# Which buffer slots the first expert weights take at the start of the mixture-of-experts stage

## The reference

```python
def first_block(...):
    ...
        mix = jnp.concatenate([o_gla, o_moba, o_mem], axis=-1)
        x = x + jnp.einsum('bse,ed->bsd', mix, w_out[l])
        x = x + hierarchical_moe(rmsnorm(x, ffn_norm_g[l]), w_router_group[l], b_router_group[l],
                                 w_router_expert[l], b_router_expert[l], w_gate[l], w_up[l], w_down[l])

    def expert_block(args):
        toks, e = args
        xb = x_pad[toks]
        hid = jax.nn.silu(xb @ w_gate[e]) * (xb @ w_up[e])
        return hid @ w_down[e]
```

## Time and profile before

| | us |
|---|---|
| median of 3 runs | 1449.39 |
| lowest and highest | 1448.79, 1451.52 |
| the profiled execution, its own time | 1451.52 |
| the profiled execution, its span | 1449.8 |
| PE busy | 1186.8 (82%) |
| DVE busy | 616.1 (42%) |
| ACT busy | 475.5 (33%) |
| mean granted TensorE clock | 0.883 |

### The profile page before, as it was taken

How to read it: one execution, slowest core, us unless ns; L and a number is a source line. 1 busy time by engine, 2 the same in 40 slices (tenths; PEclk the granted TensorE clock), 3 DMA queues, 4 the chain that set the end, 5 groups by cost and what they waited for, 6 DMA issues and landing times.

```text
span 1449.8 us, 19467 instructions
## 1 busy us (share of the span) xinstructions
PE 1186.8 (82%) x7703; PEld 875.1 (60%) x7703; DVE 616.1 (42%) x1240; ACT 475.5 (33%) x767; POOL 7.6 (1%) x54
## 2 busy tenths in 40 slices
PE   5888878667565674666887789999999888999998
PEld 5665575233232341324664438899898745999986
DVE  4564742101000010002853676655445656665543
ACT  5552611000000000002622345544433456454541
POOL 1000000000000000000000000000000000000000
PEclk9997888888897897886997678999999988999999
DMA  8543668999999999999455432965454571756520
GB/s 298 182 168 104 245 232 335 430 429 429 429 430 429 429 431 428 431 420 341 146 177 188 158 117 97 287 198 175 175 199 179 207 272 45 233 178 201 201 90 30
DMA packets 121777, 368.68 MB, mean 254 GB/s; under 512 B 9890, under 2 KB 56141, under 8 KB 110926
## 3 DMA queue, kind: packets, MB, share of 16 engines
q1 hardware_dynamic: 120604, 367.26, 66.1%
q10 hardware_dynamic: 1074, 0.08, 0.1%
HBM read 366.28 MB, written 1.05 MB: 253 GB/s over the span
## 4 chain that ended last, share of the span: by engine, by line
PE 59%; DMA 20%; DVE 12%; ACT 4%; issue 3%; SPq 1%; DVEq 0%; ACTq 0%
PE ps L1832 57%; DMA more<-in_w_up_dram 8%; DMA more<-in_w_gate_dram 6%; DMA more<-in_w_down_dram 6%; DVE st L32 2%; DVE ring_r L32 2%; PE ps L1836 2%; DVE R_c L32 2%; SPq L669 1%; DVE X_c L32 1%; DVE R_a L32 1%; DVE X_a L32 1%; ACT X_c L32 1%; DVE sc L32 1%; ACT R_a L32 1%
## 5 line engine op out<-in xcount | busy, mean ns | idle before, releaser
L1832 PE MATMUL ps<-ring,xg 128*32 128x512 f32 x640 | 141.1, 741 | 125.4 <-DMA more<-in_w_gate_dram 78.3
L1832 PE MATMUL ps<-hT_r,ring_r 128*128 128x256 f32 x864 | 243.5, 282 | 0.0
L1832 PEld LDWEIGHTS ps<-ring,xg 128*32 128x32 f32 x640 | 37.3, 133 | 222.2 <-issue 222.2
L1832 PEld LDWEIGHTS ps<-hT_r,ring_r 128*128 128x128 f32 x864 | 165.8, 192 | 0.0
L32 DVE TENSOR_TENSOR ring_r<-ring,W_c_r 128x1024 fp32r<-128x1024 f32 x94 | 115.2, 1226 | 96.3 <-ACT W_c_r L32 92.4
L1832 PE MATMUL ps<-R_c_r,W_c_r 128*128 128x256 f32 x608 | 152.7, 283 | 0.0
L32 DVE TENSOR_TENSOR ring_r<-ring,X_c_r 128x1024 fp32r<-128x1024 f32 x88 | 107.8, 1225 | 95.2 <-ACT X_c_r L32 92.3
L1832 PE MATMUL ps<-R_c_r,X_c_r 128*128 128x256 f32 x576 | 147.7, 284 | 0.0
L1832 PE MATMUL ps<-more,xg 128*32 128x512 f32 x384 | 135.6, 727 | 0.0
L32 ACT ACTIVATE W_c_r<-ring 128x1024 fp32r<-128x1024 f32 x94 | 99.7, 1060 | 87.3 <-PE ps L1832 82.9
L32 ACT ACTIVATE X_c_r<-ring 128x1024 fp32r<-128x1024 f32 x88 | 93.3, 1061 | 89.5 <-PE ps L1832 84.3
(11 more groups left out here) (280 smaller groups left out, 1899.8 us busy)
## 6 DMA issues: line engine op xcount, KB each, us to landing
ring<-in_ada_w_dram SPq DMA_DIRECT2D x24, 2048.0 KB, 8.1
ring<-in_w_gate_dram SPq DMA_DIRECT2D x20, 2048.0 KB, 16.2
ring<-in_w_up_dram SPq DMA_DIRECT2D x20, 2048.0 KB, 18.5
ring<-in_w_down_dram SPq DMA_DIRECT2D x20, 2048.0 KB, 17.6
more<-in_w_gate_dram SPq DMA_DIRECT2D x12, 2048.0 KB, 26.4
more<-in_w_up_dram SPq DMA_DIRECT2D x12, 2048.0 KB, 27.5
more<-in_w_down_dram SPq DMA_DIRECT2D x12, 2048.0 KB, 26.3
ring<-in_ffn_gate_dram SPq DMA_DIRECT2D x22, 1024.0 KB, 5.9
```

The costliest lines, as they stand in the source:

```text
L1832: return pe.matmul(out, lhsT, rhs, start=start, stop=stop, skip_group_check=True)
```

## The change

The list that hands out slots is no longer written out at load 12 but derived from the rotation as it stands there. At that point `order` is [2, 3, 4, 0, 1]. The list before was [2, 0, 1, 5, 3, 4, 6, 7]; the new expression gives [4, 0, 1, 5, 2, 3, 6, 7].

```diff
@@ -380,7 +380,7 @@
         last_in = {}
         for k in range(nload):
             if k == m0:
-                order = [2, 0, 1, NR, 3, 4] + list(range(NR + 1, NR + MR))
+                order = order[2:] + [NR] + order[:2] + list(range(NR + 1, NR + MR))
             if k == m1_ + 1:
                 order = [z for z in order if z < NR]
             z = order.pop(0)
```

## The result

The changed kernel takes 1463.09 us (median of 4 runs, 1461.24 to 1464.96), the kernel before 1449.87 us beside it. The ratio is 1.0094, with a 95% interval of 1.0073 to 1.0115: it is slower by 13.6 us, between 10.6 and 16.7; the two medians are 13.2 us apart. The forecast was 1461.8 us in a range of 1459.0 to 1466.5. Of all 31 executions of the changed kernel 30 lie between 1461.24 and 1470.54 us with a median of 1462.6, and one, in a slow state with a mean granted clock of 0.70, took 1596.32 us and is left out.

What follows compares the result with a forecast made beforehand. The DMA stream of expert weights was taken to bound the kernel; 25.0 us of loads less 12.5 us idle gave +12.4 us, so 1463.9 us for the profiled execution and 1461.8 us as median, range 1459.0 to 1466.5.

Steps and rivals of the forecast that it cites:

- What bounds the kernel: Expert stage, about 240 to 660 us: the DMA stream alone sets the pace, at 4.875 us a load.
- All eight loads start where load 17 did: Loads 12 to 19 all go out from 196.2 us, the end of the output projection, as one block.
- 25.0 us for five loads, less 12.5 us of idle time: Start of the expert stream: five more loads at 4.99 us, less the idle stretch 213.1 to 225.6 us, giving 12.4 us.
- rival 1: The block of eight strided loads runs as slowly as loads from 143 to 163 us: +15 to +17 us; 10%.
- PE doesn't wait in group 0 before `down(0)`: Expert group 0: both first phases run unmoved; `down(0)` is the first late phase, at 259.5 us instead of 253.6.
- The whole delay is carried to the end: From `down(0)` to the kernel's end, every phase stays 12.4 us late, with no gap to catch up in.
- one of the prediction's own signs: The prediction would be wrong if the shifts at 300 us and at the end differed by over 2 us.
- The Trainium skill's HBM limit: Loads from HBM: at about 358 GB/s five cost 29.3 us, a delay of about 17 us; left out of the sum.
- Hidden: Start of the expert stage: slots fill before PE needs them, so the late start costs +0, within 2.9 us; 3%.
- Partly carried: Expert stage or step into the next block takes up some of the delay, leaving +3 to +9 us; 5%.
- Faster through relief between 143 and 196 us: Attention stage and projection shorten without loads beside them, by more than 12.4 us (16 us at 30%); 2%.

Runs made afterwards that it cites:

- light pair: The kernel before and the changed kernel, each with a quarter of the bytes in expert loads 20 to 103: 1289.49 and 1289.97 us.
- first_alone: Only slots 2 and 4 swapped against the kernel before, so load 12 waits for the end of the output projection: 1462.31 us.
- wait_at_2nd: Against the kernel before, the slot free only after the output projection goes to the second expert load, holding back four loads: 1461.56 us.
- wait_at_3rd: Against the kernel before, the slot free only after the output projection goes to the third expert load, holding back three: 1456.13 us, run again 1453.24.
- wait_at_5th: Against the kernel before, slots 3 and 4 swapped for loads 16 and 17, holding back only load 16: 1449.33 us.
- later_start: The changed kernel with load 12 also waiting for the routing flag, so the stream starts 16.0 us later: 1478.74 us.
- hold_17_to_flag: The kernel before with its own slots, load 17 also waiting for the routing flag, which holds back loads 17 to 19: 1455.25 us.

## Why the prediction was right

**What bounds the kernel**: right. The stage is bound by the stream; the light pair shows that without this bound the change has no cost in time that can be seen (1289.49 and 1289.97 us).

**All eight loads start where load 17 did**: right. 198.19 us, at the same point of the program; the 2 us go with the granted clock of the execution.

**25.0 us for five loads, less 12.5 us of idle time**: the mechanism is right, and the first term was too small. In the landing times of the traces, load 19 landed 17.9 us after the issue of load 17 before (196.24, 214.1), and 44.8 us after that of load 12 now (198.19, 243.0). The difference is 26.9 us instead of 25.0. Nearly all of the 1.9 us lies in one step: the fifth load of the block lands 6.7 us behind the fourth, the others 4.8 to 5.1 us apart. So it isn't rival 1, whose price was a slow pace of the whole block, 5.6 us a load. The second term was right: load 20 landed 17.5 us behind load 19 before and 4.9 us behind it now, 12.6 us less. A third term was not in the sum: load 24 landed 5.8 us behind load 23 before and 4.9 now, which gives 0.9 us back. 26.9 - 12.6 - 0.9 = 13.4 us.

**PE doesn't wait in group 0 before `down(0)`**: wrong by a little. Load 19 landed 44.8 us behind the first issue, for 43.8 foreseen (240 for 196.2; the 2 us from last byte to landing in this figure are 1.0 us in the kernel before, 213.1 and 214.1), and PE was there earlier, as three quarters of `up(0, 0)` took 5.36 us at a higher granted clock and 7.05 before. It waited 2.04 us. It cost the full kernel nothing, as the stream had loads queued; in the light pair it is the 2 us in group 0. `down(0)` began at 262.6, or 260.7 with the 2 us of the start taken off, for 259.5.

**The whole delay is carried to the end**: right nearly to the end of the stage, not exact to a us. By one of the prediction's own signs it would be wrong: the shift at 300 us is 15.4 us and that of the span 12.2, 3.2 us apart, and the sign was set at 2 us. The account of the two profiled spans:

| step | us |
|---|---|
| output projection ends later (granted clock, not the change) | +2.0 |
| first phases bound by the stream, net | +13.4 |
| taken back by the last expert load (15.4 to 14.5) | -0.9 |
| taken back from there to the first product of the next block | -2.2 |
| the rest | -0.1 |
| span | +12.2 |

Most of the 0.9 us lies at the stream's end: the net delay is still 13.1 us at the last load but one, and the last expert load landed 5.6 us behind it before and 5.0 us after. The last 2.2 us are the clock again. The kernel before ran this piece mostly at the lower level, and the changed one did the same 84 matmuls in 27 us at a higher share:

```profile
659.00:688.00 29.00, 20.04 (x84) 13.47 (x84) 7.42 (x18) 7.70 (x13) 0.00 (x0) 0.59 0.90 333
```
```profile
673.00:700.00 27.00, 17.02 (x84) 11.39 (x84) 7.42 (x18) 7.70 (x13) 0.00 (x0) 0.68 0.99 364
```

Most of the difference is in one product, right behind those on the last expert load, before and after:

```profile
662.62 6.04 PE L1832 MATMUL ps<-sT,yv 128*128 128x256 f32 x16 [0.79 <-ACT yv L32]
676.52 3.88 PE L1832 MATMUL ps<-sT,yv 128*128 128x256 f32 x16 [0.81 <-ACT yv L32]
```

It took 6.04 us at a granted clock of 0.61 and 3.88 us at 1.00. It also took 3.88 us in first_alone, wait_at_2nd, both profiles of wait_at_3rd, wait_at_5th and later_start, and 5.87 us in hold_17_to_flag. So it was the profiled execution of the kernel before that was slow here, and any span compared with it comes out some 2 us short: the second profile of wait_at_3rd, 3.3 us late in the stream, has a span only 0.2 us longer than the kernel before.

From 700 us to the end the two have the same granted clock (0.92) and at the end the same distance as at 700. The medians are 13.2 us apart for a net delay of the stream of 13.4, so in them these pieces about even out; which runs had which of them can't be told without their traces. The total came out within 1.3 us of the forecast, with a first term 1.9 us too small of which 0.9 came back by a term that was not in the sum. That part is luck.

**The Trainium skill's HBM limit** ("DMA: Bandwidth & Descriptors", section "Bandwidth", about 358 GB/s a core, which the same section gives for both cores of a pair streaming) would have made the delay 17 us. The trace after disagrees as the one before did: 403 to 430 GB/s in its windows from 200 us on.

**The rivals.** Slow block: not what the landing times show, as told above. Hidden: refuted in this kernel by the time, and true of the light pair. Partly carried: 0.9 us of 15.4 at the end of the stage; the 2.2 us at the step into the next block belong to the execution of the kernel before. Faster through relief between 143 and 196 us: first_alone's router products began 0.1 us earlier than in the kernel before, without any load beside the attention stage, and the kernels with and without early loads start them in the same range.

## What to carry to other kernels

Where one stage is bound by a stream of loads, its start is worth the loads that are through before it becomes continuous, less the idle time that they would otherwise have filled; loads held back within that idle time are free, beyond it each costs its whole transfer time (here one, three, four and five loads: none, 3.4, 8.5 and 13.4 us). A queue that issues in order is only as early as the latest condition at its head, so the slot that comes free last belongs to the last of the early loads. And an idle stretch of a bounding stream, behind full slots, is where one more slot pays (3.9 us here).

## What was not expected of the hardware

SP's queue took three of the expert loads cut into quarters in 0.4 to 0.5 us each, and then needed 3 to 6 us for each further one (from 199.78 us on), about the pace at which loads completed. The block of eight also had one uneven step: the fifth landed 6.7 us behind the fourth, the others 4.8 to 5.1 us apart. The step doesn't belong to the fifth place. In hold_17_to_flag the second load of its block landed 6.5 us behind the first, at 226.4 us, and in later_start the third 6.6 us behind the second, at 231.6 us; in the changed kernel, first_alone, wait_at_2nd and both profiles of wait_at_3rd it is the load that landed at 225 to 228 us. So it seems to go with the time, around 225 us, and not with the place in the block; in the kernel before the idle stretch ends there. What makes it stays open; a like step of 6.4 us comes once more in each of these seven traces, at load 64.

One and the same kernel had profiled spans 7.2 us apart, and the granted clock of PE from about 820 us on is the only difference found between them. A difference under some 5 us in this kernel is told from the traces, stage by stage, better than from a few total times.
